# Two transformer blocks in one launch: late expert scores in 512-column products, identity products in waits, the branch passage and the expert layer's first and last steps in another order

## The reference

```python
def hybrid_layer(x, c, positions, ...):                      # first block
    sh1, sc1, g1, sh2, sc2, g2 = split(silu(c) @ w_ada + b_ada, 6)
    h = rms_norm(x, norm1_g) * (1 + sc1) + sh1
    qa, ka, va, qb, kb, vb, gl = split(h @ w_in)
    oa = dilated attention of 12 heads in 3 groups (q, k normed, rope), mixed over the groups
    ob = rms_norm(differential attention of 8 heads, subln_g)    # two softmaxes per head
    mixed = gate_a * (oa @ w_proj_a) + gate_b * (ob @ w_proj_b)  # gates = sigmoid(gl + b_gate)
    x = x + g1 * (mixed @ w_out)
    h2 = rms_norm(x, norm2_g) * (1 + sc2) + sh2
    # PEER: 8 heads, each its 16 best of 128 x 128 experts, softmax over them
    return x + g2 * sum over chosen e of gate_e * gelu(u_e . h2) * v_e

def second_block(x, mem, ...):
    x = x + parallel_mixer(rms_norm(x))          # a short convolution and a gated linear recurrence
    x = x + memory_cross_attention(rms_norm(x), rms_norm(mem))
    x = x + hierarchical_moe(rms_norm(x))        # best of 4 groups, 2 best of its 4 experts
    return rms_norm(x, final_norm)               # expert: (silu(t @ w_gate) * (t @ w_up)) @ w_down
```

## Time and profile before

| | before |
|---|---|
| median of 3 runs | 1890.0 us (1889.41 to 1891.11) |
| the profiled execution | 1889.28 us, its span 1887.6 us |
| mean granted TensorE clock | 0.984 |
| PE busy | 1828.9 us (97%) |
| DVE busy | 1316.7 us (70%) |
| ACT busy | 911.8 us (48%) |
| POOL busy | 77.8 us (4%) |
| moved by DMA | 404.94 MB, mean 215 GB/s |

### The profile page before, as it was taken

How to read it: one execution, slowest core, us unless ns; L and a number is a source line. 1 busy time by engine, 2 the same in 40 slices (tenths; PEclk the granted TensorE clock), 3 DMA queues, 4 the chain that set the end, 5 groups by cost and what they waited for, 6 DMA issues and landing times.

```text
span 1887.6 us, 25804 instructions
## 1 busy us (share of the span) xinstructions
PE 1828.9 (97%) x10066; PEld 1568.2 (83%) x10066; DVE 1316.7 (70%) x1857; ACT 911.8 (48%) x1013; POOL 77.8 (4%) x101
## 2 busy tenths in 40 slices
PE   8999998999999999999999999989999899999997
PEld 4778766888898889999999999889979778888885
DVE  5779787569998565455554555567874688888887
ACT  2553564311234444444444444456644467667665
POOL 0000000100000431110000000000000000000000
PEclk9999999999999999999999999989999799999999
DMA  7655464433446885665555555555343579898884
GB/s 306 246 182 197 155 238 136 151 132 137 162 168 228 245 279 200 204 219 200 187 190 185 193 179 194 183 182 181 135 157 139 200 296 360 318 357 332 321 351 156
DMA packets 61697, 404.94 MB, mean 215 GB/s; under 512 B 8129, under 2 KB 8417, under 8 KB 15281
## 3 DMA queue, kind: packets, MB, share of 16 engines
q1 hardware_dynamic: 51904, 371.22, 53.5%
q0 software_dynamic: 5968, 20.82, 3.9%
q10 hardware_dynamic: 3746, 11.83, 1.9%
HBM read 391.25 MB, written 12.58 MB: 214 GB/s over the span
## 4 chain that ended last, share of the span: by engine, by line
PE 86%; DVE 7%; DMA 3%; ACT 3%; issue 1%; SPq 0%; DVEq 0%; ACTq 0%
PE ps L2321 23%; PE ps L2323 22%; PE ps L2322 22%; PE ps L2427 7%; PE ps L2724 3%; DMA raw<-in_stream_dram 1%; DMA BIG<-in_stream_dram 1%; ACT whi L692 1%; PE ps L2900 1%; DVE wlo L1238 1%; PE ps L2437 1%; PE ps L2783 1%; PE ps L2558 0%; PE ps L2937 0%; PE ps L2537 0%
## 5 line engine op out<-in xcount | busy, mean ns | idle before, releaser
L1238 DVE TENSOR_TENSOR wlo<-raw,whi 128x2048 fp32r<-128x2048 f32 x179 | 410.2, 2292 | 324.9 <-ACT whi L692 324.7
L692 ACT ACTIVATE whi<-raw 128x2048 fp32r<-128x2048 f32 x179 | 343.1, 1917 | 390.9 <-PE ps L2323 381.8
L2321 PE MATMUL ps<-thi,whi 128*128 128x256 f32 x1056 | 301.2, 285 | 2.5 <-DVE tlo L1255 2.3
L2322 PE MATMUL ps<-tlo,whi 128*128 128x256 f32 x1056 | 300.4, 284 | 0.0
L2323 PE MATMUL ps<-thi,wlo 128*128 128x256 f32 x1056 | 300.4, 284 | 0.0
L2321 PE MATMUL ps<-whi,phi 128*128 128x512 f32 x608 | 239.1, 393 | 7.6 <-DVE plo L1829 6.1
L2322 PE MATMUL ps<-wlo,phi 128*128 128x512 f32 x608 | 237.8, 391 | 0.0
L2323 PE MATMUL ps<-whi,plo 128*128 128x512 f32 x608 | 237.3, 390 | 0.0
L2321 PE MATMUL ps<-whi,thi 128*128 128x512 f32 (+1 forms) x576 | 227.0, 394 | 4.2 <-DVE wlo L1238 3.2
L2323 PE MATMUL ps<-whi,tlo 128*128 128x512 f32 (+1 forms) x576 | 223.1, 387 | 0.0
L2322 PE MATMUL ps<-wlo,thi 128*128 128x512 f32 (+1 forms) x576 | 222.9, 387 | 0.0
(11 more groups left out here) (411 smaller groups left out, 2648.0 us busy)
## 6 DMA issues: line engine op xcount, KB each, us to landing
raw<-in_stream_dram SPq DMA_DIRECT2D x259, 1024.0 KB, 4.8
BIG<-in_stream_dram SPq DMA_DIRECT2D x84, 1024.0 KB, 6.7
BIG<-g_spill POOLq DMA_DIRECT2D x64, 128.0 KB, 4.9
BIG<-in_stream_dram SPq DMA_DIRECT2D x2, 2048.0 KB, 16.6
spare<-in_stream_dram SPq DMA_DIRECT2D x4, 1024.0 KB, 6.4
g_spill<-H ACTq DMA_DIRECT2D x4, 1024.0 KB, 4.8
g_spill<-MOD ACTq DMA_DIRECT2D x4, 1024.0 KB, 4.8
MID<-in_gains_dram POOLq DMA_DIRECT2D x7, 512.0 KB, 4.0
```

The costliest lines, as they stand in the source:

```text
L692: nc.scalar.activation(whi[:, u % 2, :], raw_of(u), ACT.Copy).then_inc(unit_hi, 1)
L1238: nc.vector.tensor_tensor(wlo[:, u % 2, :], raw_of(u), whi[:, u % 2, :].bitcast(f32), ALU.subtract).then_inc(unit_split, 1)
L2321: nc.tensor.matmul(out, ahi, bhi, start=start, stop=False)
L2322: nc.tensor.matmul(out, ahi, blo, start=False, stop=False)
```

## The change

Five parts:

1. **Late scores.** `thi` and `tlo` become the two halves of one buffer, `tboth`, interleaved by chunk, so that one product takes both as its moving factor (512 columns). A block is now `whi` x both and `wlo` x `thi` (256 columns, added to the first half). The sum of the halves is in two banks of 1024 numbers; VectorE's new `summed(i)` adds the halves of each before ScalarE's Gelu, which now reads and writes SBUF.
2. **Branch passage.** `hi(U_PA)` stands behind ScalarE's head loop, `hi(U_PB)` behind the square root for ob, `tr_high(T_OB)` before `hi(U_PA + 2)`. VectorE's `lo(U_PB)` stands before the last modulation rows. TensorE's wait for ob's values stands before one bank instead of at the start, and its transposes of `T_OB` no longer wait for the low parts of the groups before.
3. **Identity products.** `run_on(bank, n)` multiplies the identity matrix by a constant, in whole fp32, 256 columns, into a bank that nobody reads: 9 before the first values, 8 before the mixer's transposes, 3 before cross attention's, 3 before the router's, 5 before the counts, 3 before the gather.
4. **Expert layer, first step.** VectorE makes the slots of block 1 and `to_tok` right before the first hidden rows, the other slots right after them. `gate_up(s, 0)` waits for ScalarE's silu of the step before, not for VectorE's hidden rows.
5. **Last step.** `hidden_T(19)` stands inside the down products of step 18; the last unit is used in the order that completes half 0 of the result first; copies, scatter, additions, squares and means go by halves, into four banks of their own.

Lines that only declare the semaphore `scores_summed` or reshape a view are left out here, and eight spaces of indentation.

```diff
@@ -168,4 +168,4 @@
 H = sb("H", [P, TT, D])
-thi = sb("thi", [P, DC, S], f32r)
-tlo = sb("tlo", [P, DC, S], f32r)
+tboth = sb("tboth", [P, DC, 2, S], f32r)
+thi, tlo = tboth[:, :, 0, :], tboth[:, :, 1, :]
 with nc.sbuf_tensor("MOD", [P, 6 * D], f32) as mod_tensor:
@@ -893,4 +894,3 @@
             b_exp(h + 2)
-        else:
-            hi(U_PA + h + 2 - B_HEADS)
+    hi(U_PA)
     b_rows(B_HEADS - 1)
@@ -900,6 +900,7 @@
     nc.scalar.activation(ob_stat, ob_stat, ACT.Sqrt).then_inc(ob_std, 1)
+    hi(U_PB)
-    hi(U_PA + 2)
     tr_high(T_OB)
+    hi(U_PA + 2)
     hi(U_PB + 2)
@@ -991,4 +992,4 @@
-        used(at_u(i), 2 * off)
-        nc.scalar.activation(act_s[i % 2], ps[:, 4 + i % 2, :], ACT.Gelu).then_inc(gelu_done, 1)
+        act.wait_ge(scores_summed, i - EARLY + 1 + off)
+        nc.scalar.activation(act_s[i % 2], act_s[i % 2], ACT.Gelu).then_inc(gelu_done, 1)
         gated_high(i, off)
@@ -1214,7 +1215,9 @@
     hidden_high(STEPS - 1)
-    rows_out(N_BLK - 1)
+    for h in range(2):
+        act.wait_ge(m_used, 2 * M_UNITS + h - 1)
+        nc.scalar.activation(y_hi[:, half_cols(h)], ps[:, 3 + h, :], ACT.Copy).then_inc(y_copied, 1)
     root_table()
-    for t in range(TT):
-        for h in range(2):
-            half_square(6, t, h, X, y_added, 4 * (N_BLK - 1) + 2 * t + h + 1)
+    for h in range(2):
+        for t in range(TT):
+            half_square(6, t, h, X, y_added, 4 * (N_BLK - 1) + 2 * h + t + 1)
@@ -1638,4 +1641,4 @@
                                 ).then_inc(rows_ready, 1)
-    ada_out((10, 11), (6, 7), ada_full, 4)
     lo(U_PB)
+    ada_out((10, 11), (6, 7), ada_full, 4)
@@ -1843,2 +1846,9 @@
         weighted_low(i, source=early_out(i))
+    def summed(i, off=0):
+        used(at_u(i), 2 * off)
+        got = ps[:, 4 + 2 * (i % 2):6 + 2 * (i % 2), :].rearrange("p j (a t) -> p j t a", a=2)
+        nc.vector.tensor_reduce(act_s[i % 2].rearrange("p (j t) -> p j t", j=2), got, axis=AX.X, op=ALU.add
+                                ).then_inc(scores_summed, 1)
     lo(at_u(EARLY))
@@ -1846,3 +1856,5 @@
     lo(at_v(EARLY))
+    summed(EARLY)
     gated(EARLY)
+    summed(EARLY + 1)
     lo(at_u(EARLY + 2))
@@ -1856,2 +1868,3 @@
                 i = first + k
+                summed(i, 2 * r)
                 lo(at_u(i + 1), 4 * r)
@@ -2266,15 +2279,4 @@
     m_low(3)
-    for b in range(1, N_BLK):
-        slots_of(b)
-    mark(nc.vector.tensor_reduce(over1, over4, axis=AX.X, op=ALU.add))
-    settle()
-    mark(nc.vector.tensor_scalar(over1, over1, 6.0 * PER_GRP, None, ALU.mult))
-    settle()
-    nc.vector.tensor_copy(over_at, over1).then_inc(over_ready, 1)
     dve.wait_ge(dest_full, TT)
     mark(nc.vector.tensor_scalar(dest_T, ps[:, 4, 0:S], pidx, None, ALU.subtract))
-    settle()
-    for b in range(N_BLK):
-        nc.vector.tensor_scalar(to_tok[:, b, :], dest_T, float(SLOTS * b), None, ALU.is_equal
-                                ).then_inc(toks_ready, 1)
     for s in range(STEPS):
@@ -2294,3 +2296,16 @@
             gate_low(m_in(1), 1)
+            slots_of(1)
+            settle()
+            for k in range(N_BLK):
+                nc.vector.tensor_scalar(to_tok[:, k, :], dest_T, float(SLOTS * k), None, ALU.is_equal
+                                        ).then_inc(toks_ready, 1)
         hidden(s)
+        if s == 0:
+            for k in range(2, N_BLK):
+                slots_of(k)
+            mark(nc.vector.tensor_reduce(over1, over4, axis=AX.X, op=ALU.add))
+            settle()
+            mark(nc.vector.tensor_scalar(over1, over1, 6.0 * PER_GRP, None, ALU.mult))
+            settle()
+            nc.vector.tensor_copy(over_at, over1).then_inc(over_ready, 1)
         if a == 2 and b + 1 < N_BLK:
@@ -2304,11 +2319,14 @@
     m_low(m_down(STEPS - 1))
-    m_low(m_down(STEPS - 1) + 1)
     hidden_low(STEPS - 1)
+    m_low(m_down(STEPS - 1) + 1)
     rows_low(N_BLK - 1)
-    add_rows(N_BLK - 1, 0)
-    add_rows(N_BLK - 1, 1)
-    for t in range(TT):
-        half_mean(6, t)
+    for h in range(2):
+        for t in range(TT):
+            dve.wait_ge(y_back, 4 * (N_BLK - 1) + 2 * h + t + 1)
+            nc.vector.tensor_tensor(X[:, t, half_cols(h)], X[:, t, half_cols(h)], ps[:, (5, 0)[t] + h, :], ALU.add
+                                    ).then_inc(y_added, 1)
+            if h:
+                half_mean(6, t)
     for t in range(TT):
-        dve.wait_ge(y_added, 4 * (N_BLK - 1) + 2 * t + 2)
+        dve.wait_ge(y_added, 4 * (N_BLK - 1) + 2 + t + 1)
         half_rows(6, t, X, out_ready)
@@ -2324,2 +2342,7 @@
+    def run_on(bank, times):
+        for _ in range(times):
+            nc.tensor.matmul(ps[:, bank, 0:S], ident[:, :], iota[:, :], start=True, stop=True)
     def arrived(u, off=0):
@@ -2346,3 +2369,4 @@
                     pe.wait_ge(rows_ready, ROWS[t] - TT + tokens.start // P + 1)
-                pe.wait_ge(tr_lo, g - 1)
+                if t == T_OA:
+                    pe.wait_ge(tr_lo, g - 1)
             blocks = [(c, tt) for c in range(chunks.start, chunks.stop)
@@ -2444,2 +2468,4 @@
         for m, bank in enumerate(banks):
+            if bank == 5:
+                pe.wait_ge(b_out, 2 * TT * B_HEADS)
             if g == 1:
@@ -2634,3 +2660,2 @@
     pe.wait_ge(ada_free, 3)
-    pe.wait_ge(b_out, 2 * TT * B_HEADS)
     ada_rest(1, (6, 7, 5))
@@ -2696,5 +2721,17 @@
-        if i >= 2:
-            pe.wait_ge(gelu_done, i - 1 + off)
-        block_T(ps[:, 4 + i % 2, :], u, uoff)
+        if i >= EARLY + 2:
+            pe.wait_ge(scores_summed, i - EARLY - 1 + off)
+        arrived(u, uoff)
+        s = u % 2
+        for fb in range(2):
+            out = ps[:, 4 + 2 * (i % 2) + fb, :]
+            for c in range(DC):
+                cols = slice(c * 256 + fb * P, c * 256 + (fb + 1) * P)
+                both = tboth[:, c, :, :].rearrange("p a t -> p (a t)")
+                if c == DC - 1:
+                    nc.tensor.matmul(out[:, 0:S], wlo[:, s, cols], thi[:, c, :], start=False, stop=False)
+                last = nc.tensor.matmul(out, whi[:, s, cols], both, start=c == 0, stop=c == DC - 1)
+                if c < DC - 1:
+                    nc.tensor.matmul(out[:, 0:S], wlo[:, s, cols], thi[:, c, :], start=False, stop=False)
+        last.then_inc(unit_used, 1)
@@ -2732,2 +2769,3 @@
+    run_on(2, 9)
     pe.wait_ge(gelu_done, EARLY)
@@ -2762,2 +2800,3 @@
+    run_on(7, 8)
     transposes(T_MIX, H)
@@ -2815,2 +2854,3 @@
+    run_on(7, 3)
     transposes(T_HX, H)
@@ -2883,2 +2924,3 @@
+    run_on(7, 5)
     pe.wait_ge(grp_ready, 1)
@@ -2909,2 +2951,3 @@
+    run_on(6, 3)
     gather(0)
@@ -2947,11 +2990,15 @@
             u = m_down(s) + k
+            ends = s == STEPS - 1 and k == 1
             pe.wait_ge(m_lo, 2 * (u + 1))
-            for c in range(2):
+            for c, h in ((0, 0), (1, 0), (0, 1), (1, 1)) if ends else ((0, 0), (0, 1), (1, 0), (1, 1)):
                 rows = slice((2 * k + c) * P, (2 * k + c + 1) * P)
-                for h in range(2):
-                    cols = slice(c * D + h * 512, c * D + (h + 1) * 512)
-                    last = mm3(ps[:, 3 + h, :], phi[:, s % 2, rows], plo[:, s % 2, rows],
-                               m_whi[u % W_RING][:, cols], m_wlo[u % W_RING][:, cols],
-                               a == 0 and k == 0 and c == 0, a == PER_GRP - 1 and k == 1 and c == 1)
-            last.then_inc(m_used, 2)
+                cols = slice(c * D + h * 512, c * D + (h + 1) * 512)
+                last = mm3(ps[:, 3 + h, :], phi[:, s % 2, rows], plo[:, s % 2, rows],
+                           m_whi[u % W_RING][:, cols], m_wlo[u % W_RING][:, cols],
+                           a == 0 and k == 0 and c == 0, a == PER_GRP - 1 and k == 1 and c == 1)
+                if ends and (c, h) == (1, 0):
+                    last.then_inc(m_used, 1)
+            last.then_inc(m_used, 1 if ends else 2)
+            if s == STEPS - 2 and k == 0:
+                hidden_T(STEPS - 1)
@@ -2974,3 +3021,3 @@
         if s:
-            pe.wait_ge(m_hid, s)
+            pe.wait_ge(m_silu, s)
         gate_up(s, 0)
@@ -2987,6 +3034,9 @@
             scatter(b - 1, 1)
-    hidden_T(STEPS - 1)
     down(STEPS - 1)
-    scatter(N_BLK - 1, 0)
-    scatter(N_BLK - 1, 1)
+    for h in range(2):
+        pe.wait_ge(y_split, 2 * (N_BLK - 1) + h + 1)
+        for t in range(TT):
+            back, at = ps[:, (5, 0)[t] + h, :], to_tok[:, N_BLK - 1, t * P:(t + 1) * P]
+            nc.tensor.matmul(back, at, y_hi[:, half_cols(h)], start=True, stop=False)
+            nc.tensor.matmul(back, at, y_lo[:, half_cols(h)], start=False, stop=True).then_inc(y_back, 1)
```

11 lines of the change are left out of this document (6 added, 5 removed).

## The result

| | before | after |
|---|---|---|
| median (4 runs each) | 1890.55 us (1889.41 to 1894.14) | 1871.82 us (1871.05 to 1874.71) |
| ratio | | 0.9894, 95% interval 0.9877 to 0.9912 |
| profiled execution | 1889.28 us, span 1887.6 | 1871.05 us, span 1869.3 |
| mean granted clock | 0.984 | 0.991 |
| instructions | 25804 | 24560 |

The account below looks back on a forecast made before the run. The prediction took TensorE's own work to bound the kernel (86% of the chain that ended last). Its terms summed to -26.6 us, from 1889.3 to 1862.7, stated as 1863 us, range 1853 to 1875.

Parts of the forecast that it names:

- Late products: Late scores: one 512- and one 256-column product replace three of 256 in each block; 9.2 us less over 46 pairs.
- The sum: Late scores: VectorE's adding of the halves takes 2.05 us, hidden in steady pairs, so nothing lost there.
- First late pair: First late scores: sum and Gelu lie uncovered on the path, 2.7 us more; a possible clock fall behind adds 1.2.
- Branch passage: Branch passage: earlier splits start TensorE's products on U_PB at 297.8 instead of 304.92; 5.0 us less, VectorE late next.
- Identity products: Before first values, mixer, cross attention and router to gather: filled waits cost nothing and keep the clock up; 12.4 us less.
- Router: Router to gather: filled waits raise the clock, 5.8 us less; router products in some 3.5 us.
- Rival 1: Mixer, cross attention, router: filled pauses don't hold the clock, so 10.8 us of gain go; 1874 us, chance 0.17.
- First step: Expert layer's first step: the 1.9 us wait goes, but slot tables delay the next subtractions; net 0.4 us less.
- last step: Expert layer's last step: TensorE's waits at the end shrink and the closing chain starts earlier; 3.5 us less.

Follow-up runs that it names:

- no_fill: The changed kernel without any identity product: 1876.08 us, ratio 0.9906 to the kernel before the change.
- again: The changed kernel run once more without any edit: 1868.92 us, ratio 0.9872 to the kernel before the change.
- no_first: The changed kernel with the expert layer's first step put back as it was before: 1871.87 us, ratio 0.9899 to the kernel before the change.

## Why the prediction was right, and where it was wrong

The direction and the range held; 18 of 26.6 us came. The two largest terms gave less than forecast, and the branch passage and both edits of the expert layer gave more; the size of the whole is in part that balance. By its steps:

- **Late products, -9.2.** Measured 6.2 to 6.4. The mechanism is right (a product's fixed share is 12 ns in groups), the size was cut by 4 ns for each pair of alternating widths. That was named as the unknown, and "both widths keep their pace in long rows of their own kind" was the argument that failed.
- **The sum.** I priced it at 2.05 us by the row that reads with a stride; it takes 1.22 (46 of them, 56.3 us), the price of the row without one. Steady pairs are free, as said.
- **First late pair, +2.7 and +1.2.** Wait of 2.77 for 0.72 (+2.05, since the sum is shorter), and the clock at 0.50 for the 3.4 us behind. Shown: with the sum first, 3.5 us come back.
- **Branch passage, -5.0.** 6.6 by the two traces (0.5 of it ahead of 257 us, so 6.1 in the passage), 7.0 by the medians when it is taken back. TensorE's products on U_PB start at 303.73 in a trace that lies 5.8 late from 257 us on, so at 297.9 on the clock of the kernel before; 297.8 was worked out. What was missed: the clock had been low twice inside this passage.
- **Identity products, -12.4.** This is the step that failed. The trace before and the trace after seem to give 9.2 (1.6, 2.2, 1.6 and 3.8), but taking the filling out costs 7.2 us by the medians and 2.2 by the two traces. The sum treated one profiled execution's falls as the kernel's own: each term was "the clock was low here, so it will be high". Without filling, the next profile had other falls in the same four places, so filling a wait is worth the lower clock's price times how often it falls. The price was sized too high too: in "no_fill" 3.4 us of low clock in the mixer cost 0.2, and of the 2.8 at the first values 2.4 did not last. And "all fit, and they cost nothing" was wrong before the counts, where the clock was low already: there the text itself gave the case (they take twice that and overshoot), and it came, 1.9 us.
- **Router.** Rival 1 held here: the 32 narrow products took 5.03 us, with the clock falling among them, where 3.5 were forecast. It held once elsewhere: behind filled waits the mixer's first products ran at 1.00 in eleven profiles of twelve and at 0.50 for 3.4 us in one ("First step as before"), cross attention's at 1.00 in all twelve. The Trainium skill (TensorE: Matmul & The Clock Gate, Part 4) says that transposes don't count as busy for the full clock. The eleven profiles don't show that, and the twelfth, where the clock fell right behind 16 transposes, doesn't rule it out.
- **Given back, not foreseen: 2.** With the lead at 5 us behind the first values, TensorE waited 0.72 us at 629.80 and 1.26 at 696.70 for plo, behind a split that waited for its weights (timeline of ScalarE, changed kernel):

```profile
624.81 1.92 ACT L693 ACTIVATE whi<-raw 128x2048 fp32r<-128x2048 f32 x1 [4.10 <-DMA raw<-in_stream_dram]
```

  The first values had been costed against the wait in front of them alone. Whether these waits are the transfers' own rate I did not test; they stood in "again" too (0.46 and 1.36 us), and without filling there was less lead to lose.
- **First step, -0.4, and last step, -3.5.** 1.0 and 4.1 by the table; taken back, 1.4 and 3.6 by the traces.
- **Chance.** -6.6 at 212 and +3.3 at 354 are falls of the clock in work that the change leaves alone. They took 3.3 us from the profiled execution; a run without the first stood at 1865.48.

The parts taken back one by one on one chip (0.8, 7.2, 7.0) with the two read from traces (3.6, 1.4) make 20.0 of the 24.2 us between "again" and the kernel before on that chip.

## What to carry to other kernels

When TensorE's clock is seen low behind a pause, look at the granted clock of several executions before you price it: a fall is a chance, and the price is the chance times the loss. The loss is no fixed share of the stretch at the lower clock: 3.4 us of it cost 0.2 in the mixer of "no_fill" and 1.5 in that of "no_first". Fill a wait only as far as the work fits at the lower clock too. And when a reduction or any new link is put into a loop with slack, cost the first pass by itself: the steady state was free, and one line's order in the first pass held 3.5 us.

## What was not expected of the hardware

- A reduction in PSUM that adds numbers 256 apart takes as long as one that reads side by side: 1.22 us for 1024 numbers (first row), not the 2.05 of the strided one in SBUF (which adds eight numbers for each result, not two; the two places were not compared at one shape).
- 512- and 256-column products in turn take 0.352 us together ((11.09 - 5.46) / 16, with the values' 5.46 as before), in groups 0.348, so about 4 ns for the alternation.
- The same instructions, with the same 1.69 us wait ahead, ran at a granted clock of 0.50 for 13.6 us in one execution and at 1.00 in another. What decides it was not settled.
